# The order of SyncE's transfers in the feed-forward loops: block stores before or behind the next weight loads

## What is computed

```
def swiglu(x, w_gate, w_up, w_down):
    return (jax.nn.silu(x @ w_gate) * (x @ w_up)) @ w_down
...
    for l in range(DEPTH):
        x = layer_norm(ALPHA * x + 0.5 * swiglu(x, ffn1_w_gate[l], ffn1_w_up[l], ffn1_w_down[l]),
                       ln1_g[l], ln1_b[l])
        mix = hybrid_mixer(x, ...)
        x = layer_norm(ALPHA * x + mix, ln2_g[l], ln2_b[l])
        x = layer_norm(ALPHA * x + 0.5 * swiglu(x, ffn2_w_gate[l], ffn2_w_up[l], ffn2_w_down[l]),
                       ln3_g[l], ln3_b[l])
    return x
```

## Time and profile before

| | |
|---|---|
| median of 3 runs | 1084.87 us |
| profiled execution | 1083.67 us |
| its span | 1081.9 us |
| TensorE busy | 1072.1 us (99%) |
| VectorE busy | 772.0 us (71%) |
| ScalarE busy | 579.4 us (54%) |
| granted clock of TensorE | 0.999 |
| the DMA queue's share of 16 engines | 65.5% |
| return reads | 40, median 2.6 us from issue to landing |
| block stores | 160, median 2.8 us from issue to landing |

### The profile page before, as it was taken

How to read it: one execution, slowest core, us unless ns; L and a number is a source line. 1 busy time by engine, 2 the same in 40 slices (tenths; PEclk the granted TensorE clock), 3 DMA queues, 4 the chain that set the end, 5 groups by cost and what they waited for, 6 DMA issues and landing times.

```text
span 1081.9 us, 14282 instructions
## 1 busy us (share of the span) xinstructions
PE 1072.1 (99%) x5197; PEld 882.7 (82%) x5197; DVE 772.0 (71%) x779; ACT 579.4 (54%) x641; POOL 137.3 (13%) x137
## 2 busy tenths in 40 slices
PE   8999999999999999999999999999999999999997
PEld 6888888888888788888888888888878887888886
DVE  5756557799979775555679665677999787655566
ACT  5755654768554544444456655547774546344441
POOL 1498000000000000000006970000000000000000
PEclk9999999999999999999999999999999999999999
DMA  8877879355566486777737877775455674688761
GB/s 285 263 216 231 296 223 225 105 184 171 175 185 208 149 272 226 233 259 225 250 124 231 248 244 254 230 199 165 148 166 157 195 268 133 209 268 270 235 208 40
DMA packets 192371, 226.39 MB, mean 209 GB/s; under 512 B 31540, under 2 KB 157128, under 8 KB 192328
## 3 DMA queue, kind: packets, MB, share of 16 engines
q1 hardware_dynamic: 192328, 225.83, 65.5%
HBM read 214.26 MB, written 11.53 MB: 209 GB/s over the span
## 4 chain that ended last, share of the span: by engine, by line
PE 97%; DMA 1%; SPq 1%; DVE 1%; issue 0%; ACT 0%; DVEq 0%
PE ps L578 25%; PE ps L555 19%; PE ps L557 18%; PE ps L556 18%; PE ps L538 4%; PE ps L540 2%; PE ps L974 1%; PE ps L976 1%; PE ps L975 1%; PE ps L593 1%; DMA raw<-in_ffn_w_up 1%; PE ps L901 1%; DMA tp<-in_ln_b 0%; PE ps L686 0%; PE ps L685 0%; PE ps L684 0%
## 5 line engine op out<-in xcount | busy, mean ns | idle before, releaser
L1449 DVE TENSOR_TENSOR w_lo<-raw,w_hi 128x2048 fp32r<-128x2048 f32 x172 | 399.9, 2329 | 166.7 <-ACT w_hi L1058 165.6
L1058 ACT CAST w_hi<-raw 128x2048 fp32r<-128x2048 f32 x172 | 328.1, 1910 | 162.1 <-PE ps L578 78.9
L555 PE MATMUL ps<-w_hi,xT 128*128 128x512 f32 x848 | 331.8, 391 | 0.3 <-DVE w_lo L1461 0.2
L556 PE MATMUL ps<-w_lo,xT 128*128 128x512 f32 x848 | 330.1, 389 | 0.0
L557 PE MATMUL ps<-w_hi,xT 128*128 128x512 f32 x848 | 330.1, 389 | 0.0
L555 PEld LDWEIGHTS ps<-w_hi,xT 128*128 128x128 f32 x848 | 159.2, 188 | 36.2 <-issue 2.5
L557 PEld LDWEIGHTS ps<-w_hi,xT 128*128 128x128 f32 x848 | 159.2, 188 | 33.0
L556 PEld LDWEIGHTS ps<-w_lo,xT 128*128 128x128 f32 x848 | 159.2, 188 | 32.7
L578 PE MATMUL ps<-w_hi,rows_hi 128*128 128x512 f32 x396 | 126.6, 393 | 0.0
L578 PE MATMUL ps<-w_hi,rows_lo 128*128 128x512 f32 x396 | 125.4, 390 | 0.0
L578 PE MATMUL ps<-w_lo,rows_hi 128*128 128x512 f32 x396 | 125.2, 389 | 0.0
(11 more groups left out here) (248 smaller groups left out, 1117.1 us busy)
## 6 DMA issues: line engine op xcount, KB each, us to landing
raw<-in_ffn_w_down SPq DMA_DIRECT2D x44, 1024.0 KB, 6.6
raw<-in_ffn_w_gate SPq DMA_DIRECT2D x86, 512.0 KB, 4.1
raw<-in_ffn_w_up SPq DMA_DIRECT2D x86, 512.0 KB, 5.2
raw<-in_w_in SPq DMA_DIRECT2D x30, 1024.0 KB, 5.1
hid_dram<-qT SPq DMA_DIRECT2D x160, 64.0 KB, 2.8
qT<-hid_dram SPq DMA_DIRECT2D x40, 256.0 KB, 2.6
raw<-in_w_out SPq DMA_DIRECT2D x8, 1024.0 KB, 4.9
raw<-in_w_in SPq DMA_DIRECT2D x8, 512.0 KB, 5.0
```

What stands on the lines that cost most here:

```text
L555: mm(o, xT[:, c, 0, tok], h, start=c == UPPER_FIRST[0], stop=False, skip_group_check=True)
L556: mm(o, xT[:, c, 0, tok], w, start=False, stop=False, skip_group_check=True)
L1058: nc.scalar.copy(w_hi[s][:, :], raw[s][:, :]).then_inc(hi_made.sem, 1)
L1449: tt(w_lo[s][:, :], raw[s][:, :], f32(w_hi[s][:, :]), ALU.subtract).then_inc(lo_made.sem, 1)
```

## The change

`turn_hidden` is cut in two: `blocks_to_dram` waits for the blocks and issues the four stores, and `hidden_back` waits for the stores and issues the return read. In `step` the first now stands ahead of the load of raw2, the second where `turn_hidden` stood. Behind the loops the two are called in a row, as before.

```diff
--- before.py
+++ after.py
@@ -357,13 +357,16 @@
                 for n, v in enumerate((g, b)):
                     sp.dma_start(gb[:, n, :], v[bass.ds(l, 1)].to_broadcast([P, D])).then_inc(gb_landed.sem, 16)
 
-            def turn_hidden(l, n):
+            def blocks_to_dram(l, n):
 
                 sp.wait_ge(blocks_made.sem, blocks_made.at(l, n))
                 for a in range(4):
                     sp.dma_start(hid_dram.rearrange("g i a r -> a i g r")[a],
                                  hid_blocks[32 * a:32 * a + 32, :].rearrange("i (g r) -> i g r", g=4)
                                  ).then_inc(blocks_out.sem, 16)
+
+            def hidden_back(l, n):
+
                 sp.wait_ge(blocks_out.sem, blocks_out.at(l, n))
                 sp.dma_start(hid_turned, hid_dram.rearrange("g i a r -> (g i) (a r)")).then_inc(h_turned.sem, 16)
 
@@ -388,8 +391,9 @@
 
                 def step(i):
 
+                    blocks_to_dram(l, f * (STEPS - 1) + i - 1)
                     load(l, k0 + i * 3 - 1, gate_up(w_gate, w_up, l, 1, i * 256), 2)
-                    turn_hidden(l, f * (STEPS - 1) + i - 1)
+                    hidden_back(l, f * (STEPS - 1) + i - 1)
                     load(l, k0 + i * 3, gate_up(w_gate, w_up, l, 0, i * 256), 0)
                     load(l, k0 + i * 3 + 1, rows(w_down, l, i * 256 - 256), 1)
 
@@ -402,7 +406,8 @@
                 with sp.Fori(8, STEPS) as i:
                     step(i)
                 load(l, k0 + FFN_CHUNKS - 1, rows(w_down, l, DFF - 256))
-                turn_hidden(l, (f + 1) * (STEPS - 1))
+                blocks_to_dram(l, (f + 1) * (STEPS - 1))
+                hidden_back(l, (f + 1) * (STEPS - 1))
 
             def q_columns(l, a):
                 def parts(r):
```

## The result

The changed kernel takes 1088.0 us (median of 7 runs, 1087.63 to 1088.95), the kernel before in the same comparison 1084.69 us (7 runs). The ratio is 1.0036 with a 95% interval of 1.0026 to 1.0046: slower, by 3.3 us. The profiled execution took 1087.94 us with a span of 1086.2, against 1083.67 and 1081.9.

The account below looks back on a forecast made before the run. TensorE was taken to bound the kernel, waiting 0.11 us at most in the loops. First-step waits 0.45+3x1.01 plus restarts 4x0.15 made 4.1 us, added to the median 1084.87 for 1089.0 us; range 1084.7 to 1090.2.

Parts of the forecast that it names:

- The first rival: Return read behind raw2's weights isn't held up; not slower, 1084.9 us; chance 0.34 together with its softer form.
- softer form: Stores' longer lag is load, not place; return lands at E+5.3, just in time in all networks; within the 0.34.
- E: Time in a pass when SyncE's issue of the four block stores ends; 375.97 us in the second network's first pass.
- The second rival: Delay reaches the second step in the two networks with small parameters; up to 1.5 us more, 1090.5; chance 0.07.
- The third: Rival of a gain from blocks leaving 1 us earlier in 15 passes; at most 0.11 us, 1084.8; chance 0.04.
- the restart: TensorE's extra cost after each wait at the first down products; 0.15 us each, four times.
- the reserve: Second network's first pass: rows_lo ended at 381.82, down product began at 382.91; 1.09 us in hand.
- the fourth network's: First step of the fourth network: rows_lo ends at 917.63, product due at 916.62; late by 1.01 us.

Follow-up runs that it names:

- e7_between: Changed kernel with the return read issued between raw2's gate and up loads; 1092.06 us, ratio 1.0074 to the kernel before.
- e3_return_first: Changed kernel with the order stores, return read, then raw2's loads; 1088.58 us, ratio 1.0039 to the kernel before.
- e5_raw0_ahead: Changed kernel with raw2's loads back ahead of the stores and raw0's load moved in front of the return read; 1095.36 us, ratio 1.01 to the kernel before.
- e4_act_queue: Changed kernel with the return read issued by ScalarE on its own queue; 1096.23 us, ratio 1.0101 to the kernel before.
- e6_act_queue_old: Old order on SyncE, return read issued by ScalarE, raw0's load held until the return landed; 1106.31 us, ratio 1.0222 to the kernel before.
- e8_act_queue_held: Changed kernel's order, return read issued by ScalarE, raw0's load held until the return landed; 1095.32 us, ratio 1.0104 to the kernel before.

## Why the prediction was right

**Direction and mechanism.** Each step held: no gain, since TensorE had no wait to lose; stores that leave no sooner where SyncE waited for them; raw2's up chunk 4.5 us later; the return behind it; a wait in the first pass of the networks and 16.32 us between all later products. The first rival, a return that isn't held up, fell with its lag of 5.0 in the changed kernel. So did its softer form, which had it land at E+5.3 where it landed at E+6.45; e7_between goes against the reason behind that form, since as much was under way there and the lag was 3.5. Of the rule quoted there (the Trainium skill, "DMA: Bandwidth & Descriptors", "Two DMAs through the same engine are not ordered") the first half fits the row, descriptors starting in order; the completion ahead of earlier writes, which it allows, no run here shows for the return: it landed 0.67 us behind the weights. The second rival did not come about in the changed kernel (`rows_lo` of the second step ended in time everywhere, by 0.5 us in the first network). Waits at that place did come in e3_return_first, though not by the way of the rival: in the first network `rows_lo` of the first step was early there (29.96) and raw2's residual late (VectorE began it at 34.44, in the changed kernel at 32.52), and the rest of VectorE's work moved with it. The third was bounded by 0.11 us, and nothing was gained.

**Sizes.** For the second network: return issued at E+1.45 (forecast E+1.4; E=375.94), up chunk's lag 4.9 (5.0), return 0.67 behind it (0.75), landing at E+6.45 (E+6.6), `rows_lo` 1.36 behind that (1.35). Together this is 0.14 us less than forecast, and `rows_lo` came 0.83 us late instead of 1.01 (the wait of 0.98 less the 0.15 of restart). The term that was undersized is the restart. I took 0.15 us from one place, the second matmul's delay. Measured are 0.15 from the end of `rows_lo` to the first matmul and 0.26 to 0.29 more within the product, 0.4 in all and 1.7 over the four networks instead of 0.6. Seen from the other side, the reserve was overstated by about as much: the chain has the product begin at 382.91, but TensorE's timeline has its first matmul at 382.75, and 0.15 ahead of that is when `rows_lo` had to end, so 0.8 us were in hand and not 1.09.

The forecast sum was 4.1 us. The four networks cost 5.0 in the traced execution (0.72 and 4.30), the spans differ by 4.3, the medians by 3.3 (interval 2.8 to 5.0). So the mechanism was right, but that the sum lies so near the difference of the spans is in part luck: the forecast was 0.9 short of what the waits and restarts took, and an earlier start gave 0.76 back.

**What fell.** Of the single terms, the fourth network's: `rows_lo` was 1.2 us late instead of 1.0, because the up chunk's lag was 5.3 there and the return landed at E+6.8. In the first network it was late by 0.31 instead of 0.45 us (the wait of 0.46 holds 0.15 of restart). And the expectations of time for most of the later runs were too low. In e3_return_first, e7_between and the two runs that hold raw0, a transfer that was moved or held back ran out of a reserve of its own, which I had bounded too loosely; in e5_raw0_ahead it was the restart and the granted clock, in e4_act_queue waits in second and last steps as well as in the first.

## What to carry to other kernels

When transfers are reordered, list for each how late it may be, not only how early it could go. Here the stores that were moved forward had no use for their new place in 25 of 40 passes, and the loser was neither they nor the weights that changed places with them, but the small read right behind; moving it out of the way again (e3_return_first, e7_between) only handed the wait on to the weights. And read a reserve at the first pass of a loop as well as in the settled ones: 1.1 us there (0.8 by the reading above) against 6.0 in a settled one (`rows_lo` ended at 458.50, the product began at 464.51 in the kernel before) decided the whole result.

No version here beats the kernel before. The best, the new order with the old first pass, ties with it (0.9994, interval 0.9985 to 1.0003), as it must where TensorE idles for 0.1 us in the loops.

## What the runs showed of the hardware that I had not expected

- A second queue is no way past the weights: the 256 KB of the return took 2.6 us alone (e6_act_queue_old) and 4.8 with 1 MB issued just before it on the other queue (e8_act_queue_held), landing 0.66 us behind that in the first pass of the second network; on one queue it was 0.67.
- In e5_raw0_ahead TensorE's granted clock fell to its lower level (0.50, that is 1.2 of 2.4 GHz) behind two of four waits of 1.8 to 2.1 us, and a product then took 7.34 us, 1.6 more than behind the other two. In e6_act_queue_old it fell to 0.50 behind waits of 3.98 and 3.40 us, but not behind one of 1.91. It fell behind none of the changed kernel's waits, of up to 1.35 us, where it stayed at 0.999 on average. Why some waits of 1.8 to 2.1 us were spared and others not is open. A reserve missed by 2 us can so cost 4.
- A product that starts after a wait costs more than the wait, even at full clock: 0.15 us between the end of the awaited piece and the first matmul, and 5.70 us instead of 5.44 in the chain. By TensorE's timeline, 0.13 of this 0.26 lies in slower matmuls (from the first of the product to the first behind it 383.90 to 389.47, 5.57 us, against 382.75 to 388.19, 5.44, in the kernel before). The rest is the first matmul's length of 0.39 us, of which 0.16 lie under the matmul ahead when there is one.
